# The block compression of a hybrid decoder's first mixer: blocks stationary in four column quarters, weights moving

## The chip, the cores and the metric

The kernel runs on one core of one Trainium2 chip. The core has a matrix engine (TensorE, PE in the profile, whose weight loads are listed as PEld), a vector engine (VectorE, DVE), a scalar engine (ScalarE, ACT), GpSimd (POOL) and a queue engine (SyncE, SP) that issues the DMA transfers. The metric is the device time of one execution in microseconds (us). Everything is computed in float32.

## The reference

Two layers over 256 tokens of width 1024. Layer 0 mixes with RWKV-7 heads and sparse-attention heads side by side, layer 1 with Mamba-2; each is followed by a mixture of 32 experts. The change is in layer 0, in the compressed branch of the sparse attention. It turns overlapping blocks of 32 tokens (a new block each 16 tokens, so 15 blocks) of the key and of the value columns into one vector each, by a two-layer network:

```python
n_cmp = (s_ - CMP_BLOCK) // CMP_STRIDE + 1        # 15
blk_idx = np.arange(n_cmp)[:, None] * CMP_STRIDE + np.arange(CMP_BLOCK)[None, :]

def compress(t, pe, w1, b1, w2):
    blocks = kv_heads(t)[:, blk_idx] + pe[:, None, :]
    flat = blocks.transpose(0, 1, 3, 2, 4).reshape(b_, n_cmp, hk, CMP_BLOCK * d)
    return jax.nn.silu(flat @ w1 + b1) @ w2       # w1: 2048 x 128, w2: 128 x 64

k_cmp = partial_rope(compress(kc, pe_k, w1_k, b1_k, w2_k), cmp_end)
v_cmp = compress(vc, pe_v, w1_v, b1_v, w2_v)
```

`flat @ w1` is a contraction over 32 positions `l` of a block times 64 channels, for 2 KV heads times 15 blocks = 30 rows and 128 hidden units, once for keys and once for values.

## The kernel before

The program of each engine is written out by hand, one after another, in blocks for the first mixer ("hyb"), the experts, the second mixer ("ssm") and the experts again. Engines meet only at semaphores: `at(...)` is the count that a named mark has reached. PSUM banks are taken in turn: `take(pe, ..., pool=left)` hands out banks 0 to 3 in rotation, and waits until the bank's last job has been read. `right` is the other four banks ("sums" in the profile).

In the first mixer the input projection is cut into six groups of columns. Their weights pass through two halves of `wr`, each refilled by the SP queue when the group two before it is done (mark `("group", g)`). `by_channels` (line 1140) computes 256 columns of a group, with the weights stationary and the 256 tokens of `uT` moving: 16 products over 8 steps. The second half of group 3 (`("feat", NK, 1)`) is written out apart, since it is mixed with the compression.

The compression's operands: `w1` holds the first-layer weights as [64 channels, l, 128], keys on partitions 0 to 63 (`x` = 0), values on 64 to 127 (`x` = 1); it lies in `front`, under which name the profile shows it. `blk` holds the blocks plus their position terms as [64 channels, l, 30], laid out likewise, and is made by four additions on VectorE. For each of the 32 positions and both `x` one product has `w1` of the position stationary (64 rows, 128 columns) and the 30 columns of `blk` moving, accumulated in one bank for each `x` as [128 hidden, 30]. After each pair of positions stands one of the 16 products of the projection (line 1189). ScalarE then applies the sigmoid and the bias (lines 994 and 996, `hsg` and `hid`), VectorE multiplies the two (line 698), and PE multiplies by `w2` (line 1207), behind the low-rank products of line 1200. ScalarE's copy of the projection's bank into `z` (line 932) stands behind lines 994 and 996 in its queue.

What follows in the mixer is one long chain on PE, VectorE and ScalarE. The expert weights come through a ring of slots, `raw`; the SP queue loads ahead into it wherever the mixer's own tiles have been given up (`load_ahead`), after waits for marks of the mixer.

Of the kernel before, what the change touches and what calls it, by code (L numbers as in the profile page):

```python
# [11 lines left out]
ACT = mybir.ActivationFunctionType  # L12
AX = mybir.AxisListType

P = 128
D = 1024
SEQ = 256
HALVES = SEQ // P
KD = D // P
# [4 lines left out]
HEADS, HD = 8, 64  # L24
# [3 lines left out]
KV = 2  # L28
# [5 lines left out]
NCMP, CBLK, CSTR = 15, 32, 16  # L34
# [24 lines left out]
def columns(spec):  # L59

    at, out = 0, {}
    for name, n in spec:
# [4 lines left out]


CHK = 64
NCHK = SEQ // CHK  # L70
LEVELS = range(1, 6)

# [1 line left out]
                         ("ident64", CHK), ("slots", 128), ("slots_s", 128), ("key", 32),  # L74
                         ("headones", 2), ("headsum", 32), ("headspread", 512), ("scankeep", 256), ("strict_upto", 2 * CHK),
                         ("causal", 256), ("cmpok", 30), ("cos", 16), ("sin", 16), ("ccos", 8), ("csin", 8),
                         ("lev0", CHK), ("levT", 6 * CHK)])

SHARED = CONST["headones"][0]

# [9 lines left out]
def shape_tables():  # L90
    c = np.zeros((P, NCONST), np.float32)

    def put(name, v):
        at, n = CONST[name]
        c[:, at:at + n] = v.reshape(P, n)

    i = np.arange(P)
    put("ident", np.eye(P))
    put("before", (i[:, None] < i[None, :]).astype(np.float32))
    put("upto", (i[:, None] <= i[None, :]).astype(np.float32))  # L100
    put("ones", np.ones((P, P)))
    head = np.arange(HEADS)
    put("headones", (i[:, None] // HD == np.arange(2)[None, :]).astype(np.float32))
    put("headsum", np.stack([head[None, :] == 2 * m + i[:, None] // HD for m in range(4)], 1).astype(np.float32))
    spread = np.zeros((P, 4, P), np.float32)
    for m in range(4):
        spread[:HEADS, m, :] = head[:, None] == 2 * m + i[None, :] // HD
    put("headspread", spread)
    loc, pos = i[:, None] % CHK, np.arange(CHK)
    put("ident64", (loc == pos[None, :]).astype(np.float32))  # L110
    put("strict_upto", np.concatenate([loc < pos[None, :], loc <= pos[None, :]], 1).astype(np.float32))
    put("slots", np.tile(np.arange(P) % CAP, (P, 1)))
    put("slots_s", np.tile(np.arange(P) % CAP_S, (P, 1)))
    e = np.arange(EXPERTS)
    put("key", np.tile(np.maximum(FIXED - e, 0) * FIRST_KEY - e, (P, 1)))
    put("scankeep", np.tile((np.arange(SEQ) % CHK != 0), (P, 1)))
    put("causal", np.concatenate([np.zeros((P, P)), np.where(i[None, :] <= i[:, None], 0, NEG)], 1))
    tok = i[:, None] + P * np.arange(HALVES)[None, :]
    end = np.arange(NCMP) * CSTR + CBLK - 1
    put("cmpok", (end[None, None, :] <= tok[:, :, None]).astype(np.float32))  # L120
    inv = np.power(np.float32(500000.0), -np.arange(ROPE_HALF, dtype=np.float32) * np.float32(2.0 / 16))
    ang = tok[:, :, None].astype(np.float32) * inv
    put("cos", np.cos(ang)), put("sin", np.sin(ang))
    cang = np.zeros((P, ROPE_HALF), np.float32)
    cang[:NCMP] = end[:, None].astype(np.float32) * inv
    put("ccos", np.cos(cang)), put("csin", np.sin(cang))
    lev = np.stack([(loc >> (l + 1) == pos[None, :] >> (l + 1)) & (loc >> l & 1 == 1)
                    & (pos[None, :] >> l & 1 == 0) for l in range(6)], 1).astype(np.float32)
    put("lev0", lev[:, 0])
    put("levT", np.tile(lev[:CHK].transpose(2, 1, 0), (2, 1, 1)))  # L130
    return c

# [15 lines left out]
def build(nc, a, known, new):  # L148
# [3 lines left out]
    pe_done, act_done, dve_done, pool_done = sem("pe_done"), sem("act_done"), sem("dve_done"), sem("pool_done")  # L152
    sems = {"pe": pe_done, "act": act_done, "dve": dve_done, "pool": pool_done}
    E = {k: Count(k, new) for k in sems}
    PE, AC, DV, PO = E["pe"], E["act"], E["dve"], E["pool"]

    def at(*mark):

        who, n = known.get(mark, ("pe", 1))
        return sems[who], n  # L160
# [11 lines left out]
    def C(name, rows=P):  # L172
        o, n = CONST[name]
        return cst[0:rows, o:o + n] if o < SHARED else cst_hyb[0:rows, o - SHARED:o - SHARED + n]

    def FT(name, rows=P):
        o, n = FEAT[name]
        return feat[0:rows, o:o + n]
# [8 lines left out]
    def take(pe, *job, pool=tuple(range(8))):  # L187

        n = turn["n"].get(pool, 0)
        turn["n"][pool] = n + 1  # L190
        b = pool[n % len(pool)]
        if turn["last"][b] is not None:
            pe.wait_ge(*at("read", *turn["last"][b]))
        turn["last"][b] = job
        new[("bank",) + job] = ("pe", b)
        return bank[b]

    def bank_of(*job):
        return bank[known.get(("bank",) + job, ("pe", 0))[1]]
# [224 lines left out]
    hyb = Area(AREA)  # L424
# [5 lines left out]
    cT = hyb("cT", [P, KV, SEQ])  # L430
    w2 = hyb("w2", [P, 2, HD])
    pe_ = hyb("pe_", [P, CBLK])
    blk = hyb("blk", [P, CBLK, KV * NCMP])
    hid, hsg = hyb("hid", [P, 2, KV * NCMP]), hyb("hsg", [P, 2, KV * NCMP])
    cmpk = hyb("cmpk", [NCMP, KV, 2, HD])
    crp = hyb("crp", [NCMP, 4, 2 * KV * ROPE_HALF])
# [34 lines left out]
    uT = hyb("uT", [P, KD, SEQ])  # L471
# [6 lines left out]
    amt, dcy = R4("amt"), R4("dcy")  # L478
    wr = hyb("wr", [P, 2, KD, BANK])
    cst_hyb = hyb("cst_hyb", [P, NCONST - SHARED])  # L480

    flat = lambda ap, *dims: ap.rearrange("p " + " ".join(dims) + " -> p (" + " ".join(dims) + ")")
    u = front[:, 0:2 * D].rearrange("p (t d) -> p t d", t=HALVES)
    junk = front[:, 3 * D:4 * D]
    w1 = front[:, :].rearrange("p (l m) -> p l m", m=P)
# [47 lines left out]
    with nc.Block(name="hyb", no_gpsimd_drain=True) as block:  # L533
# [44 lines left out]
        def _(dve):  # L578
# [90 lines left out]
            nc.vector.memset(eps_n[:, 2:3], 1e-5)  # L669
            nc.vector.memset(eps_n[:, 3:4], 0.0)  # L670
            nc.vector.memset(z[:, :, 0:1], 0.0)
            nc.vector.memset(zlo[:, :, 0:1], 0.0).then_inc(dve_done, DV.one(("consts",)))
            dve.wait_ge(s_ld["ident"], 16)
            dve.wait_ge(s_ld["x"], 16)
# [93 lines left out]
            lev0, levT = C("lev0"), C("levT").rearrange("p (l s) -> p l s", s=CHK)  # L768
# [123 lines left out]
            for t in range(HALVES):  # L892
                rows = slice(0, P) if t else slice(CHK, P)
# [25 lines left out]
        def _(act):  # L919
            A = nc.scalar  # L920
# [8 lines left out]
            def columns_read(g, j):  # L929

                act.wait_ge(*at("feat", g, j))
                A.copy(z[:, 4 * g + 2 * j:4 * g + 2 * j + 2, 1:SEQ + 1],
                       bank_of("feat", g, j)[:, :].rearrange("p (c t) -> p c t", c=2)).then_inc(
                    act_done, AC.one(("read", "feat", g, j)))
# [25 lines left out]
            for t in range(HALVES):  # L960
                act.wait_ge(*at("nsa", 1, t))
                b = bank_of("nsa", 1, t)
# [17 lines left out]
            for br in range(2):  # L980
# [8 lines left out]
            A.activation(gts[:, :, :], nsav[:, :, 4 * HD:4 * HD + 24], ACT.Sigmoid).then_inc(act_done,  # L989
                                                                                          AC.one(("gates",)))  # L990
            columns_read(NK, 0)
            for x, n in enumerate("kv"):
                act.wait_ge(*at("hid", "mm", x))
                A.activation(hsg[:, x, :], bank_of("hid", "mm", x)[:, 0:KV * NCMP], ACT.Sigmoid,
                             bias=FT("b1_" + n)).then_inc(act_done, AC.one())
                A.activation(hid[:, x, :], bank_of("hid", "mm", x)[:, 0:KV * NCMP], ACT.Identity,
                             bias=FT("b1_" + n)).then_inc(act_done, AC.one(("hsg", x)))
                new[("read", "hid", "mm", x)] = ("act", AC.n)
            columns_read(NK, 1)
            act.wait_ge(*at("zz", 7))  # L1000
            for c in range(4):
                i = A.activation(kk2[:, c, :], k4[:, c, :], ACT.Square, scale=FT("k_k")[:, c:c + 1])
            i.then_inc(act_done, AC.one(("kk2",)))
            for name, dst, bias in (("wup", dcy, "w0"), ("aup", amt, "a0")):
                for j in range(2):
                    act.wait_ge(*at(name, j))
                    for c in (2 * j, 2 * j + 1):
                        A.activation(dst[:, c, :], bank_of(name, j)[:, (c % 2) * SEQ:(c % 2 + 1) * SEQ], ACT.Sigmoid,
                                     bias=FT(bias)[:, c:c + 1]).then_inc(
# [105 lines left out]
        def _(pe):  # L1115
            T = nc.tensor
            left, right = (0, 1, 2, 3), (4, 5, 6, 7)
# [46 lines left out]
            for x, (o, m) in enumerate(LO):  # L1164
                b = take(pe, "lo", x, pool=left)
                for k in range(KD):
                    i = T.matmul(b[0:m, 0:SEQ], wr[:, 0, k, o:o + m], uT[:, k, :], start=(k == 0), stop=(k == KD - 1))
# [7 lines left out]
                turned(("kT", br), [two(t, HEADS + 4 * br + 2 * g) for g in range(KV) for t in range(HALVES)], left)  # L1175
            by_channels(3, NK, 0)
            pe.wait_ge(*at("blk", 1, 1))
            bs = [take(pe, "hid", "mm", x, pool=left) for x in range(2)]
            w = weights(3)
            b = take(pe, "feat", NK, 1, pool=left)  # L1180
            for l in range(CBLK):
                for x in range(2):
                    i = T.matmul(bs[x][:, 0:KV * NCMP], w1[HD * x:HD * x + HD, l, :], blk[HD * x:HD * x + HD, l, :],
                                 start=(l == 0), stop=(l == CBLK - 1))
                    if l == CBLK - 1:
                        i.then_inc(pe_done, PE.one(("hid", "mm", x)))
                if l % 2:
                    c, step = divmod(l // 2, KD)
                    i = T.matmul(b[:, c * SEQ:(c + 1) * SEQ], w[:, step, (2 + c) * P:(3 + c) * P], uT[:, step, :],
                                 start=(step == 0), stop=(step == KD - 1))  # L1190
            i.then_inc(pe_done, PE.one(("feat", NK, 1)))
            new[("group", 3)] = ("pe", PE.n)
            pe.wait_ge(*got("par"))
# [1 line left out]
            for x, name in enumerate(("wup", "aup")):  # L1195
                lo = slice(W_RANK * x, W_RANK * (x + 1))
                for j in range(2):
                    b = take(pe, name, j, pool=right)
                    for c in (2 * j, 2 * j + 1):
                        i = T.matmul(b[:, (c % 2) * SEQ:(c % 2 + 1) * SEQ], par[lo, c * P:(c + 1) * P], lo3[lo, 0, :],  # L1200
                                     start=True, stop=True)
                    i.then_inc(pe_done, PE.one((name, j)))
            pe.wait_ge(*at("hid", 1))
            b = take(pe, "cmp", pool=left)
# [6 lines left out]
            b = take(pe, "ksum", pool=right)  # L1211
# [1639 lines left out]
```

## Time and profile before

| | |
|---|---|
| median of 3 runs | 1397.82 us (1396.78 to 1404.53) |
| the profiled execution | 1401.55 us |
| its span, first to last instruction | 1399.7 us |
| mean granted TensorE clock (1 is full) | 0.959 |
| PE busy | 1272.6 us, 91% of the span |
| DVE, ACT busy | 410.1 us, 269.3 us |
| moved by DMA | 464.10 MB, mean 332 GB/s |

The profile was taken of one execution, the runs are others; the profiled one was 3.7 us above the median. A float32 product shows as two records of PE (MATMUL) and two of PEld (LDWEIGHTS). A form such as "64*128 64x30" is the stationary operand (rows * columns), then the moving one (rows x columns). A record's own time is its latency, and the records of a run overlap: the rate at which PE works is read from where one group of records starts and the next one does.

### The profile page before, as it was taken

How to read it: one execution, taken by the hardware profiler on the slowest of the kernel's cores; microseconds unless marked ns; L12 is line 12 of the kernel's file. 1: busy time of each engine (PE TensorE's matmuls, PEld its weight loads, DVE VectorE, ACT ScalarE, POOL GpSimd, SP SyncE). 2: the span in 40 equal slices, each digit the busy share in tenths (PEclk: the TensorE clock that was granted, in tenths of full speed). 3: DMA queues.
4: the chain of work that ended last, by engine and by line, in shares of the span. 5: the costliest groups of instructions: out<-in, count | busy, mean ns of one | idle time of the engine just before them, and what ended most of it. 6: DMA issues, size and time to landing. Idle time of an engine off the chain costs nothing. (4 is left out here: it accounts for less than half of the span.)

```text
span 1399.7 us, 21009 instructions
## 1 busy us (share of the span) xinstructions
PE 1272.6 (91%) x8852; PEld 717.3 (51%) x8852; DVE 410.1 (29%) x1024; ACT 269.3 (19%) x535; POOL 15.2 (1%) x18
## 2 busy tenths in 40 slices
PE   6999999899999988698989999998999999876986
PEld 3668896544444334253368788535444444333432
DVE  1236775421211211012035756315211211110212
ACT  2223341211011000010131566202111110000101
POOL 0000000000000000000000101000000000000000
PEclk9999999999999989989999999999999999997999
DMA  9511107999999999999965446757999999999996
GB/s 305 181 61 61 62 5 298 407 409 428 426 427 428 427 427 427 424 427 427 389 228 202 150 169 253 316 231 306 430 427 427 428 427 427 427 427 424 427 428 262
DMA packets 63484, 464.10 MB, mean 332 GB/s; under 512 B 8272, under 2 KB 13680, under 8 KB 34960
## 3 DMA queue, kind: packets, MB, share of 16 engines
q1 hardware_dynamic: 63376, 462.59, 80.8%
q8 instruction: 76, 1.25, 0.4%
q14 instruction: 32, 0.26, 0.0%
HBM read 461.50 MB, written 1.08 MB: 330 GB/s over the span
## 5 line engine op out<-in xcount | busy, mean ns | idle before, releaser
L1974 PE MATMUL bank<-raw,xg 128*32 128x512 f32 x1664 | 234.7, 656 | 45.3 <-DMA raw<-in_moe_w_up 39.2
L1884 DVE TENSOR_TENSOR aT<-bank,sg 128x128 f32<-128x128 f32 (+1 forms) x64 | 20.3, 317 | 558.4 <-ACT sg L1795 558.4
L1974 PEld LDWEIGHTS bank<-raw,xg 128*32 128x32 f32 x1664 | 57.6, 119 | 196.7 <-issue 123.7
L1911 PE MATMUL bank<-sel,ux 128*128 128x64 f32 (+1 forms) x896 | 118.2, 288 | 16.9 <-DVE sel L1817 12.0
L1911 PEld LDWEIGHTS bank<-sel,ux 128*128 128x128 f32 x896 | 111.0, 202 | 40.9 <-issue 26.0
L2021 PE MATMUL sums<-ys,selT 64*128 64x512 f32 x512 | 127.2, 615 | 3.3 <-DVE ys L1897 3.3
L1792 ACT COPY gus<-bank 128x512 f32<-128x512 f32 x64 | 37.5, 586 | 436.6 <-PE bank L1974 331.4
L2012 PE MATMUL bank<-raw,aT 128*32 128x512 f32 x832 | 100.0, 598 | 10.8 <-DVE aT L1884 10.8
L2021 PEld LDWEIGHTS sums<-ys,selT 64*128 64x128 f32 x512 | 44.0, 186 | 87.6 <-issue 80.7
L1955 PE MATMUL bank<-raw,xg 128*64 128x512 f32 x384 | 84.8, 594 | 0.0
L2615 PE MATMUL sums<-uT,wr 128*128 128x256 f32 x352 | 78.1, 380 | 0.0
L1897 DVE COPY ys<-bank 128x512 f32<-128x512 f32 x64 | 44.0, 688 | 111.6 <-PE bank L2012 79.8
L1985 PEld LDWEIGHTS bank<-cst,gus 128*128 128x128 f32 x416 | 50.3, 191 | 44.5 <-issue 34.9
L2615 PEld LDWEIGHTS sums<-uT,wr 128*128 128x128 f32 x352 | 66.3, 190 | 9.4 <-issue 0.7
L1985 PE MATMUL bank<-cst,gus 128*128 128x64 f32 x416 | 57.5, 281 | 4.2 <-ACT gus L1792 4.2
L1766 ACT COPY xg<-bank 128x256 f32<-128x256 f32 (+1 forms) x56 | 23.4, 418 | 178.3 <-PE bank L1911 178.3
L2615 PE MATMUL bank<-uT,wr 128*128 128x256 f32 x256 | 57.1, 381 | 0.0
L1955 PEld LDWEIGHTS bank<-raw,xg 128*64 128x64 f32 x384 | 27.5, 137 | 51.7 <-issue 50.7
L2615 PEld LDWEIGHTS bank<-uT,wr 128*128 128x128 f32 x256 | 48.0, 190 | 6.9 <-issue 0.7
L2012 PEld LDWEIGHTS bank<-raw,aT 128*32 128x32 f32 x832 | 21.7, 109 | 50.6 <-issue 30.4
L1999 PE MATMUL bank<-raw,aT 128*64 128x512 f32 x192 | 43.8, 599 | 3.0 <-DVE aT L1884 3.0
L1795 ACT ACTIVATE sg<-bank 128x128 f32<-128x128 f32 (+1 forms) x64 | 19.1, 298 | 137.7 <-PE bank L1985 114.8
(415 smaller groups left out, 1326.6 us busy)
## 6 DMA issues: line engine op xcount, KB each, us to landing
raw<-in_moe_w_gate SPq DMA_DIRECT2D x54, 2048.0 KB, 40.8
raw<-in_moe_w_up SPq DMA_DIRECT2D x54, 2048.0 KB, 45.3
raw<-in_moe_w_down SPq DMA_DIRECT2D x54, 2048.0 KB, 44.7
raw<-in_moe_w_gate SPq DMA_DIRECT2D x20, 1024.0 KB, 12.5
raw<-in_moe_w_up SPq DMA_DIRECT2D x20, 1024.0 KB, 13.5
raw<-in_moe_w_down SPq DMA_DIRECT2D x20, 1024.0 KB, 13.5
wr<-in_ssm_w_in SPq DMA_DIRECT2D x10, 2048.0 KB, 8.7
wr<-in_hyb_w_in SPq DMA_DIRECT2D x5, 2048.0 KB, 7.7
```

The costliest lines, as they stand in the source:

```text
L1766: nc.scalar.copy(dst[:, :, 4 * half:4 * half + 4, :].rearrange("p x k s -> p k x s"), bank[SIDE_BANK][:, 0:8 * n].rearrange("p (k x s) -> ...
L1792: nc.scalar.copy(gus[:, :, :], bank[GU_BANK][:, :].rearrange("p (q j) -> p j q", j=4)).then_inc(S["gus"], 1)
L1884: V.tensor_tensor(out, bank[TURN_BANK][:, 0:8 * n].rearrange("p (j x) -> p j x", j=4)[:, :, n:2 * n], gated, ALU.mult).then_inc(S["act"], 1)
L1897: V.tensor_copy(ys[:, :], bank[Y_BANK][:, :]).then_inc(S["y"], 1)
L1911: i = T.matmul(bank[SIDE_BANK][:, k * n:(k + 1) * n].rearrange("p (x s) -> p x s", x=2), ux[:, t, 4 * half + k, :], src[:, t, :, :], start ...
L1955: i = T.matmul(bank[GU_BANK][CAP * m:CAP * m + CAP, :], xg[:, odd, k, :], raw[:, slot, (k % 4) * FH:(k % 4 + 1) * FH], start=(k == 0), sto ...
L1974: i = T.matmul(bank[GU_BANK][CAP_S * c:CAP_S * c + CAP_S, :], xg_f[:, x, 4 * half + k, :], raw[:, slot, k * FH:(k + 1) * FH], start=(half ...
L1985: i = T.matmul(bank[TURN_BANK][:, j * CAP:(j + 1) * CAP], gus[:, j, :], C("ident64"), start=True, stop=True)
L1999: i = T.matmul(bank[Y_BANK][CAP * n:CAP * n + CAP, :], aT[:, j, :], raw[:, slot, jj * D + n * BANK:jj * D + (n + 1) * BANK], start=(j == 0 ...
L2012: i = T.matmul(bank[Y_BANK][CAP_S * c:CAP_S * c + CAP_S, :], aT_s[:, 2 * half + jj, :], raw[:, slot, jj * D + n * BANK:jj * D + (n + 1) * ...
L2021: i = T.matmul(bank[ACC[2 * t + n]][:, :], selT[CAP * n:CAP * n + CAP, x, t * P:(t + 1) * P], ys[CAP * n:CAP * n + CAP, :], start=False, s ...
L2615: i = T.matmul(b[:, c * SEQ:(c + 1) * SEQ], wr2[:, n % 3, k, (2 * j + c) * P:(2 * j + c + 1) * P], uT2[:, k, :], start=(k == 0), stop=(k = ...
```

## The change

The compression's two operands change places. A block matrix (64 rows, now 32 columns: 30 and two columns of zeros) is stationary, and the 128 columns of `w1` of the position move. Position `l` goes to the quarter `l % 4` of the output partitions, that is of the array's columns, so each quarter gathers 8 of the 32 positions as [32 blocks, 128 hidden]. ScalarE copies the two banks to `hid4`, and for each `x` one product of `hid4` (stationary, 128 x 128) with `fold`, four identities of 32 stacked (128 x 32), adds the quarters and turns the result to [128 hidden, 32]. The 16 products of the projection no longer stand between those of the compression: all 64 of these come first, then 8 of the projection, the two folding products, and the other 8.

```diff
+BLK = 32
-                         ("lev0", CHK), ("levT", 6 * CHK)])
+                         ("lev0", CHK), ("levT", 6 * CHK), ("fold", BLK)])
+    put("fold", (i[:, None] % BLK == np.arange(BLK)[None, :]).astype(np.float32))
-    blk = hyb("blk", [P, CBLK, KV * NCMP])
+    blk = hyb("blk", [P, CBLK, BLK])
+    hid4 = hyb("hid4", [P, 2, P])
+            nc.vector.memset(blk[:, :, KV * NCMP:BLK], 0.0)
...
             columns_read(NK, 0)
+            act.wait_ge(*at("hid", "parts"))
+            for x in range(2):
+                A.copy(hid4[:, x, :], bank_of("hid", "part", x)[:, 0:P]).then_inc(
+                    act_done, AC.one(("read", "hid", "part", x)))
+            act.wait_ge(*at("hid", "mm"))
             for x, n in enumerate("kv"):
-                act.wait_ge(*at("hid", "mm", x))
-                A.activation(hsg[:, x, :], bank_of("hid", "mm", x)[:, 0:KV * NCMP], ACT.Sigmoid,
-                             bias=FT("b1_" + n)).then_inc(act_done, AC.one())
-                A.activation(hid[:, x, :], bank_of("hid", "mm", x)[:, 0:KV * NCMP], ACT.Identity,
-                             bias=FT("b1_" + n)).then_inc(act_done, AC.one(("hsg", x)))
-                new[("read", "hid", "mm", x)] = ("act", AC.n)
+                folded = bank_of("hid", "mm")[:, BLK * x:BLK * x + KV * NCMP]
+                A.activation(hsg[:, x, :], folded, ACT.Sigmoid, bias=FT("b1_" + n)).then_inc(act_done, AC.one())
+                A.activation(hid[:, x, :], folded, ACT.Identity, bias=FT("b1_" + n)).then_inc(
+                    act_done, AC.one(("hsg", x)))
+            new[("read", "hid", "mm")] = ("act", AC.n)
             columns_read(NK, 1)
...
             pe.wait_ge(*at("blk", 1, 1))
-            bs = [take(pe, "hid", "mm", x, pool=left) for x in range(2)]
+            bs = [take(pe, "hid", "part", x, pool=left) for x in range(2)]
+            for l in range(CBLK):
+                q = slice(BLK * (l % 4), BLK * (l % 4) + BLK)
+                for x in range(2):
+                    rows = slice(HD * x, HD * x + HD)
+                    i = T.matmul(bs[x][q, 0:P], blk[rows, l, :], w1[rows, l, :], start=(l < 4), stop=(l >= CBLK - 4))
+            i.then_inc(pe_done, PE.one(("hid", "parts")))
             w = weights(3)
             b = take(pe, "feat", NK, 1, pool=left)
-            for l in range(CBLK):
-                for x in range(2):
-                    i = T.matmul(bs[x][:, 0:KV * NCMP], w1[HD * x:HD * x + HD, l, :], blk[HD * x:HD * x + HD, l, :],
-                                 start=(l == 0), stop=(l == CBLK - 1))
-                    if l == CBLK - 1:
-                        i.then_inc(pe_done, PE.one(("hid", "mm", x)))
-                if l % 2:
-                    c, step = divmod(l // 2, KD)
-                    i = T.matmul(b[:, c * SEQ:(c + 1) * SEQ], w[:, step, (2 + c) * P:(3 + c) * P], uT[:, step, :],
-                                 start=(step == 0), stop=(step == KD - 1))
+            for c in range(2):
+                for k in range(KD):
+                    i = T.matmul(b[:, c * SEQ:(c + 1) * SEQ], w[:, k, (2 + c) * P:(3 + c) * P], uT[:, k, :],
+                                 start=(k == 0), stop=(k == KD - 1))
+                if c == 0:
+                    pe.wait_ge(*at("read", "hid", "part", 1))
+                    f = take(pe, "hid", "mm", pool=left)
+                    for x in range(2):
+                        i = T.matmul(f[:, BLK * x:BLK * x + BLK], hid4[:, x, :], C("fold"), start=True, stop=True)
+                    i.then_inc(pe_done, PE.one(("hid", "mm")))
```

PE's program at the compression before the change. A row gives the line, the operation, the tiles written and read, and the output's shape; L1140 is the first half of group 3, L1183 the compression, L1189 the second half, and the pair of rows L1183 and L1189 stands 16 times.

```order
L1140 MATMUL bank<-uT,wr 128x256 x16
L1183 MATMUL bank<-blk,front 128x30 x4
L1189 MATMUL bank<-uT,wr 128x256
...
L1200 MATMUL sums<-lo_99,par 128x256 x8
L1207 MATMUL bank<-w_101,hid 15x64 x4
L1213 MATMUL sums<-exc,cst_hyb 8x256 x4
```

The same place in the changed program, where L1191 is the compression, L1197 the projection, L1203 the folding, and the following rows are the old L1200, L1207 and L1213.

```order
L1148 MATMUL bank<-uT,wr 128x256 x16
L1191 MATMUL bank<-front,blk 32x128 x64
L1197 MATMUL bank<-uT,wr 128x256 x8
L1203 MATMUL bank<-cst_hyb,hid_148 128x32 x2
L1197 MATMUL bank<-uT,wr 128x256 x8
L1214 MATMUL sums<-lo_99,par 128x256 x8
L1221 MATMUL bank<-w_101,hid 15x64 x4
L1227 MATMUL sums<-exc,cst_hyb 8x256 x4
```

The 64 products of the compression now stand in one piece instead of 16, and the projection's 16 in two pieces; nothing behind them moved.

ScalarE's program at the same place, before.

```order
L932 COPY z<-bank 128x2x256
L994 ACTIVATE hsg<-bank,feat 128x30
L996 ACTIVATE hid<-bank,feat 128x30
L994 ACTIVATE hsg<-bank,feat 128x30
L996 ACTIVATE hid<-bank,feat 128x30
L932 COPY z<-bank 128x2x256
L1002 ACTIVATE exc<-zz,feat 128x256 x4
```

And in the changed program.

```order
L936 COPY z<-bank 128x2x256
L998 COPY hid_148<-bank 128x128 x2
L1003 ACTIVATE hsg<-bank,feat 128x30
L1004 ACTIVATE hid<-bank,feat 128x30
L1003 ACTIVATE hsg<-bank,feat 128x30
L1004 ACTIVATE hid<-bank,feat 128x30
L936 COPY z<-bank 128x2x256
L1010 ACTIVATE exc<-zz,feat 128x256 x4
```

Two copies are new ahead of the four activations. VectorE has one more small instruction, a fill of `blk` at its start. The SP queue has the same transfers in the same order behind the same waits; only the one table transfer that brings `fold` is wider, 1744 columns for 1712.

## Rows read from the trace of the kernel before

**Rows 1.** The page's part 1, and its DMA slices (busy tenths of 40).

```profile
PE 1272.6 (91%) x8852; PEld 717.3 (51%) x8852; DVE 410.1 (29%) x1024; ACT 269.3 (19%) x535; POOL 15.2 (1%) x18
DMA  9511107999999999999965446757999999999996
```

**Rows 2.** Stretches (us): length, busy by engine, clock, DMA share, GB/s.

```profile
60.00:68.00 8.00, 8.00 (x45) 6.89 (x43) 0.72 (x2) 5.44 (x9) 0.00 (x0) 1.00 0.75 264
68.00:87.04 19.04, 19.04 (x161) 13.10 (x160) 1.60 (x4) 1.11 (x5) 0.00 (x0) 1.00 0.00 1
87.04:96.00 8.96, 7.46 (x36) 4.12 (x35) 7.05 (x19) 6.66 (x16) 0.00 (x0) 0.72 0.68 235
230.00:700.00 470.00, 424.71 (x2692) 194.31 (x2692) 94.92 (x288) 52.98 (x120) 0.00 (x0) 0.96 1.00 421
```

**Rows 3.** What the SP queue waited for up to 260 us: total, times, longest.

```profile
SPq L293 <- PE bank L1189: 27.4, 1, 27.4
SPq L373 <- PE sums L1287: 21.6, 1, 21.6
SPq L373 <- DVE mixn L647: 13.4, 1, 13.4
```

**Rows 4.** PE's timeline at the compression: start, duration, group, count, idle before.

```profile
60.96 7.07 PE L1140 MATMUL bank<-uT,wr 128*128 128x256 f32 x32
67.97 0.63 PE L1183 MATMUL bank<-blk,front 64*128 64x30 f32 x8
68.53 0.70 PE L1189 MATMUL bank<-uT,wr 128*128 128x256 f32 x2
69.16 0.63 PE L1183 MATMUL bank<-blk,front 64*128 64x30 f32 x8
...
86.42 0.70 PE L1189 MATMUL bank<-uT,wr 128*128 128x256 f32 x2
87.05 2.96 PE L1200 MATMUL sums<-lo,par 32*128 32x256 f32 x16
...
92.05 3.57 PE L1213 MATMUL sums<-exc,cst_hyb 128*8 128x256 f32 x8 [1.50 <-ACT dcy L1008]
```

**Rows 5.** PE's timeline at other places, where tiles of other shapes run.

```profile
104.76 1.96 PE L1280 MATMUL bank<-kcT,qT 64*128 64x15 f32 x32
136.26 1.98 PE L1309 MATMUL sums<-front,qk 64*64 64x128 f32 x64
...
186.59 1.10 PE L1346 MATMUL sums<-kp,kk 64*64 64x64 f32 x32
187.52 1.10 PE L1346 MATMUL sums<-kk,kp 64*64 64x64 f32 x32
...
204.61 3.71 PE L1431 MATMUL sums<-wr,kk 64*64 64x128 f32 x64
...
306.59 3.62 PE L1974 MATMUL bank<-raw,xg 128*32 128x512 f32 x32
...
312.05 1.10 PE L1985 MATMUL bank<-cst,gus 128*128 128x64 f32 x8
312.99 1.95 PE L1911 MATMUL bank<-sel,ux 128*128 128x64 f32 x16
```

**Rows 6.** ScalarE's timeline behind the compression.

```profile
86.52 0.29 ACT L994 ACTIVATE hsg<-bank,feat 128x30 f32<-128x30 f32 x1 [17.86 <-PE bank L1183]
...
87.04 0.29 ACT L996 ACTIVATE hid<-bank,feat 128x30 f32<-128x30 f32 x1
87.21 0.60 ACT L932 COPY z<-bank 128x512 f32<-128x512 f32 x1
```

**Rows 7.** The page's group of ScalarE reads of 128 columns: busy, mean ns.

```profile
L1795 ACT ACTIVATE sg<-bank 128x128 f32<-128x128 f32 (+1 forms) x64 | 19.1, 298 | 137.7 <-PE bank L1985 114.8
```

**Rows 8.** Two-us stretches of PE: length, busy, clock, DMA share, GB/s.

```profile
92.00:94.00 2.00, 1.95 (x5) 0.50 1.04 401
98.00:100.00 2.00, 2.00 (x11) 1.00 0.00 0
```

## The prediction

> **What bounds the kernel now.** Three views were read in turn: the page for the whole, the stretches for each stage, and PE's timeline for the place of the change. The page has PE busy for 91% of the span and DMA busy at nine tenths or more from the seventh slice to the twentieth, and again in the last twelve [rows 1]. So the experts are DMA's: from 230 to 700 us its share is 1.00 at 421 GB/s [rows 2]. The change lies before that, in the first mixer, where between 68 and 87 us PE is busy in each of the 19.04 us, DMA moves nothing, and VectorE and ScalarE have 1.60 and 1.11 us of work [rows 2]. PE alone sets the time there.
>
> Does a gain there reach the end? The SP queue shows it. The refill of `wr` for the last group waits 27.4 us for line 1189; the first load-ahead waits 21.6 us for line 1287, the large one 13.4 us for `mixn`, a late result of the mixer [rows 3]. Each transfer behind the change is released by work behind the change, so the whole DMA-bound stage starts earlier by what the mixer gains, and ends earlier by as much. The hybrid weights of group 4 came in the stretch from 60 to 68 us (DMA share 0.75) and wait for nothing here [rows 2]; needed some 8 us sooner, they are still there. I count the carry at 1 us per us.
>
> **What is removed.** The mixed piece runs from 67.97 to 87.05 us, 19.08 us [rows 4]. One of its 16 periods is 69.16 - 67.97 = 1.19 us: 8 records of the compression and 2 of the projection. The projection alone goes at (67.97 - 60.96) / 32 = 219 ns a record of 256 columns [rows 4], so 0.44 us of a period are its own. The remaining 0.75 us are the compression and the changes between the tile shapes 64*128 and 128*128. Line 1280 has the same stationary shape with half the moving columns, 32 records in 1.96 us, 61 ns each at most [rows 5]. Eight of those are 0.49 us, and 0.26 us are left for two changes of shape. So the 19.08 us are about 7.0 of projection, 7.8 of compression and 4.2 of shape changes.
>
> **What is added, on PE.**
>
> The projection in two pieces: 16 products, 32 records, 7.01 us as in its first half.
>
> Two changes of shape, into the compression and out of it: 0.26 us. The folding products have the projection's shape, 128*128, and cause none.
>
> The folding: 2 products, 4 records with 128 stationary columns. The nearest rows are line 1985's, 8 records in 312.99 - 312.05 = 0.94 us, 118 ns each [rows 5]: 0.47 us. Its wait is covered: ScalarE has two copies of 128 columns, 298 ns each by its reads of that size [rows 7], 0.6 us in all, while PE has 8 products of the projection, 3.5 us. Without that cover some 0.8 us would be bare, if hand-overs of 0.1 us are allowed for at each end.
>
> The compression: 64 products, 128 records, stationary 64*32, moving 64x128. No such shape is in the trace, so its rate is bounded. Moving 128 columns takes 219 / 2 = 110 ns in one tile. How many tiles run at once is to be read from the rows that move 128 columns or more [rows 5]. Line 1431 uses only the diagonal, two tiles of 64*64: 3.71 us / 64 = 58 ns. Line 1309 uses four: 1.98 / 64 = 31 ns at most. Line 1974 has four column quarters over all 128 rows, as the change has them, and moves 512 columns in 3.62 / 32 = 113 ns, where one tile alone would need 438. So quarters do run beside each other, nearly four at a time. Eight tiles would give 110 / 8 = 14 ns. The loading of weights sets the other bound: 61 ns for 128 columns (line 1280), 187.52 - 186.59 = 0.93 us / 32 = 29 ns for 64 (line 1346), which halved gives 15 ns for 32. Both bounds from below agree at about 15 ns, but no record in these rows follows another in less than 29 ns, and I can't tell from them whether something else holds them there. I take the nearest fastest row, 29 ns: 128 x 29 = 3.7 us. Ends: 15 ns, 1.9 us, and 58 ns, 7.4 us.
>
> The Trainium skill ("TensorE: Matmul & The Clock Gate", Part 1, the section on 56 and 53.3 ns) states that starts of matmuls never come closer than about 25 ns, however little they move; its estimate for this piece would be 128 x 25 = 3.2 us and the saving 8.1 us. No row here goes below that figure, and none is narrow enough to test it.
>
> **Sum.** 7.01 + 0.26 + 0.47 + 3.7 = 11.4 us for 19.08: 7.6 us less. It is made against the profiled execution, 1401.55 us with a span of 1399.7, which would become 1393.9; the median of the runs is 3.7 us lower, 1397.82, and becomes 1390.2.
>
> **Edits at nothing.** ScalarE's copy into `z` now starts 0.1 us behind the projection's end, since the four activations before it in the queue are done during the last 3.5 us of projection; before, they ended at about 87.3, just where the copy was ready [rows 6], so this is worth 0.1 us at most. VectorE's product of `hid` and `hsg` comes earlier, and line 1207, which needs it, stood behind 2.96 us of line 1200 anyway [rows 4]. The fill of two columns of `blk` is a small instruction at the start, while VectorE waits for its first data; uncovered it would cost a few tenths. The table is 16 KB wider, 0.04 us at 421 GB/s. One more bank of the left four is taken, so later jobs use other banks; the job whose read each must await is four takes back as before, except for the next few, whose banks were read several us earlier. The idle 1.50 us ahead of line 1213 [rows 4] hangs on ScalarE's chain from the projection's end and stays.
>
> **Rivals.**
>
> *Only the two row groups overlap.* Successive products alternate between rows 0 to 63 and 64 to 127, and if quarters of the same rows waited for each other, two would run at once, as on line 1431: 58 ns, 7.4 us. Saving 3.9 us, 1393.9. Line 1974 speaks against it, with its 113 ns for 512 columns. The Trainium skill (same page, Part 3, on what overlaps) has exactly this rule: a weight load overlaps matmuls in flight only where the row group differs. By line 1974, whose four quarters share all rows, the trace disagrees. 12%.
>
> *Loading at its own rate.* The records follow at 15 ns: 1.9 us, saving 9.4 us, 1388.4. For it: 61 and 29 ns scale with the columns loaded. Against it: no row below 29. 20%.
>
> *The clock falls.* The granted clock is 1.00 over the mixed piece, and 0.72 over the 9 us behind it, which hold the idle 1.5 us and the thin products of line 1213 [rows 2, 4]. It was at the lower level, 1.2 of 2.4 GHz, at 92 to 94 and back at 98 to 100 us [rows 8]. A piece with small tiles, without the 256-column products in between, could bring the same on, and then the projection behind it runs at half speed for up to 7.5 us, 3.7 us lost: 1393.9. Against it: lines 1309 and 1346 run tiles at similar filling, four 64*64 tiles at 31 and 29 ns, and line 1309's time is that of the full clock. 10%.
>
> *Slower: the tiles don't overlap at all,* because the two records of one product meet in the same small tile. Then a record costs its 110 ns, the compression 14.1 us, and the piece 21.8 us instead of 19.08: 2.7 us longer, 1400.5. It decides from 11.3 / 128 = 89 ns a record; for over 0.5% it takes 143 ns, as with the lower clock on top (220 ns, 28 us, 1414.6). Lines 1974 and 1309 speak against it: their products have two records too. 5%.
>
> *The gain is local.* If what follows gave it back, about 1397.8. For it only that later work waits for DMA; against it, that the DMA itself waits for the mixer [rows 3]. 5%.
>
> **How the numbers follow.** The forecast, 29 ns and 1390.2, has the remaining 48%; the run scatter (two of three runs 1 us apart, one 7 us above) adds about 1.5 us on either side. The range from 1386.5 to 1395.5 takes in the bounds of the rate, 1388.4 and 1393.9, and the clock's case, and leaves out the slower, the local one and the odd high run. A measurement of this kernel tells about 0.5% from no change, which is 7.0 us: the forecast's 7.6 lies just beyond it. I count 7 in 10 of the forecast and nearly all of the fast case as faster, 0.54; the slower case splits between slower and no change, with a little for unforeseen loss, 0.05; the rest, 0.41, is within 0.5%.
>
> **What would show it.** In the changed profile: line 1191 with 128 records from about 68.0, the projection's first record 3.7 to 4.0 us later; line 1203 with no idle time before it; line 1214 starting at about 79.4 instead of 87.05; clock 1.00 up to there; the first load-ahead issued some 7.6 us earlier, and the same distance between it and the end. The forecast is wrong if line 1191 takes under 3 or over 5 us, if PE waits before line 1203, or if the distance from line 1214 to the end has changed by more than a few us, for which the clock's low stretches later in the mixer would be the first suspect.

## The result and the profile after

The changed kernel takes 1389.76 us (median of 8 runs, 1387.35 to 1392.96); the kernel before, in 8 runs beside it, 1399.32 us (1396.78 to 1404.53). The ratio is 0.9936, with a 95% interval of 0.9923 to 0.9948: faster by 9.0 us, 7.3 to 10.8; the two medians as they stand are 9.6 us apart. A second comparison on another occasion gave 1389.71 against 1398.18, ratio 0.9926 (0.9910 to 0.9943).

The profiled execution took 1387.79 us, with a span of 1386.0 us and a mean clock of 0.966. Part 1 of the page, its DMA slices, and the stretch of the change, which answer to [rows 1, 2]:

```profile
PE 1259.3 (91%) x8856; PEld 710.9 (51%) x8856; DVE 410.1 (30%) x1025; ACT 269.6 (19%) x537; POOL 15.2 (1%) x18
DMA  9520118999999999999964455858999999999996
```

```profile
68.67:78.18 9.51, 9.51 (x166) 8.21 (x165) 1.96 (x5) 1.83 (x7) 0.00 (x0) 1.00 0.01 2
```

PE's timeline at the compression (start, duration, group, count, idle before), the answer to [rows 4]:

```profile
68.67 2.03 PE L1191 MATMUL bank<-front,blk 64*32 64x128 f32 x128
70.62 3.72 PE L1197 MATMUL bank<-uT,wr 128*128 128x256 f32 x16
74.18 0.53 PE L1203 MATMUL bank<-cst_hyb,hid 128*128 128x32 f32 x4
74.55 3.70 PE L1197 MATMUL bank<-uT,wr 128*128 128x256 f32 x16
78.18 2.96 PE L1214 MATMUL sums<-lo,par 32*128 32x256 f32 x16
81.07 0.62 PE L1221 MATMUL bank<-w,hid 128*15 128x64 f32 x8
83.11 3.14 PE L1227 MATMUL sums<-exc,cst_hyb 128*8 128x256 f32 x8 [1.43 <-ACT dcy L1016]
```

The piece from the compression's first record to the low-rank products is 78.18 - 68.67 = 9.51 us, where it was 19.08 [rows 4]: 9.57 us less. The 128 records stand in 1.95 us, 15.2 ns each, the change of shape behind them included. Line 1203 has no idle time before it, and costs 74.55 - 74.18 = 0.37 us. ScalarE's timeline shows why nothing waits:

```profile
70.75 0.43 ACT L998 COPY hid<-bank 128x128 f32<-128x128 f32 x2 [1.39 <-PE bank L1191]
74.75 0.29 ACT L1003 ACTIVATE hsg<-bank,feat 128x30 f32<-128x30 f32 x1 [3.57 <-PE bank L1203]
...
78.28 0.58 ACT L936 COPY z<-bank 128x512 f32<-128x512 f32 x1 [2.72 <-PE bank L1197]
```

The copies are done at 71.18, 3 us before the folding wants them, and the copy into `z` starts as soon as the projection ends.

The two profiled executions differ by 13.7 us in their spans, more than the medians. The large load-ahead divides them (SP queue of the changed kernel; before, the same transfer was issued at 223.52):

```profile
212.23 0.33 SPq L375 DMA_DIRECT2D raw<-in_moe_w_gate  x1
```

Up to the compression the changed kernel's execution was 0.70 us later; the compression's piece gave 9.57; from there to this load it took 134.05 us for 136.47, 2.4 less; and from the load to the end 1173.8 for 1176.2, again 2.4 less. The last two are not steps of the change: the programs are the same there, and the second profiled execution of the changed kernel (changed_again, below) took 136.53 us from the piece's end to this load and 1176.5 from there, the same as the kernel before, and had a span of 1390.7. The 9.57 us of the piece are what the medians show, 9.6 us.

### The profile page after: what moved, and what is told of

Its sections match the earlier page's. It is cut to its first block and busy times, and to the rows that moved or that the text cites. A ratio compares the mean times of both kernels' runs of the same rounds, so it can differ in the third digit from the quotient of the medians.

```text
span 1386.0 us, 21021 instructions
## 1 busy us (share of the span) xinstructions
PE 1259.3 (91%) x8856; PEld 710.9 (51%) x8856; DVE 410.1 (30%) x1025; ACT 269.6 (19%) x537; POOL 15.2 (1%) x18
## 3 DMA queue, kind: packets, MB, share of 16 engines
q8 instruction: 76, 1.25, 0.4%
```

## The experiments

Theory A: the products run beside each other in as many tiles as there are row groups times column quarters, so a record costs its moving time over the number of tiles, and that is most of the gain. Rival B: the gain is the end of the mixing with the projection, and the swap of the operands adds little. Two further questions: what sets the 15 ns, and whether a us here is a us at the end. Where no time is given below, the kernel ran once, for its trace, and only the piece is compared.

**one_piece.** The kernel before, its 64 products of the old form in one piece, the projection behind:

```diff
             for l in range(CBLK):
                 for x in range(2):
                     i = T.matmul(bs[x][:, 0:KV * NCMP], w1[...], blk[...], ...)
-                if l % 2:
-                    c, step = divmod(l // 2, KD)
-                    i = T.matmul(b[:, c * SEQ:(c + 1) * SEQ], w[:, step, ...], uT[:, step, :], ...)
+            for c in range(2):
+                for step in range(KD):
+                    i = T.matmul(b[:, c * SEQ:(c + 1) * SEQ], w[:, step, ...], uT[:, step, :], ...)
```

> The kernel of before with one edit: its 64 products of the compression (w1 stationary 64*128, 30 columns moving) stand in one piece, and the 16 of the projection behind them. Theory A (the swap of the operands into eight tiles is the gain): the piece of PE from the first product of the compression to the low-rank ones takes 128 x 59 ns + 0.26 + 7.01 = 14.8 us, so 4.2 us of the 9.6 come from taking the products apart (15 pairs of shape changes at 0.28 us) and 5.4 us from the swap; run 1395 against 1399. Rival B (the mixing was the cost, the swap adds little): the piece takes about 10 us, as in the changed kernel, and the run 1390.

Measured: 1397.46 us (12 runs) against 1399.09 (17), ratio 0.9988 (0.9978 to 0.9999). PE's timeline, and its stretches (length, busy, clock, DMA share, GB/s):

```profile
67.95 8.51 PE L1181 MATMUL bank<-blk,front 64*128 64x30 f32 x128
76.38 9.29 PE L1189 MATMUL bank<-uT,wr 128*128 128x256 f32 x32
85.60 2.96 PE L1200 MATMUL sums<-lo,par 32*128 32x256 f32 x16
```

```profile
70.00:72.00 2.00, 2.00 (x42) 1.00 0.00 0
72.00:74.00 2.00, 2.00 (x40) 0.97 0.00 0
74.00:76.00 2.00, 2.00 (x22) 0.50 0.04 8
...
76.38:85.60 9.22, 9.22 (x34) 0.77 0.00 0
```

The piece took 17.65 us, not 14.8. After some 6 us of nothing but 30-column products the clock fell to its lower level of 1.2 GHz, and the projection behind them took 9.22 us where it takes 7.01. So B is refuted as the whole of the gain: taking the products apart, with the old operands, is worth 1.4 us in this trace and 1.6 in the medians. It saves the shape changes and gives most of that back through the clock. With the projection's products between the compression's the clock had stayed at 1.00 over the whole piece [rows 2]. What the end of the mixing is worth beside the swap is worked out behind mixed, below.

**one_strip, two_strips.** The changed kernel with one or two column quarters, that is two or four tiles (`n` is 1 or 2):

```diff
-                q = slice(BLK * (l % 4), BLK * (l % 4) + BLK)
+                q = slice(BLK * (l % n), BLK * (l % n) + BLK)
...
-                        i = T.matmul(f[...], hid4[:, x, :], C("fold"), ...)
+                        i = T.matmul(f[...], hid4[0:BLK * n, x, :], C("fold", BLK * n), ...)
```

> The changed kernel with all 32 positions in the first column quarter (output partitions 0 to 31); the folding then only turns 32 rows. Only the two row groups can run beside each other. Theory (time per record = moving time of one tile, 107 to 110 ns, over the tiles that run at once): 54 ns a record, 6.9 us for the 128. Rival (the rate is set by the loading of 32 columns, and the quarters don't matter): 15 ns, 2.0 us.

> The changed kernel with the positions in two column quarters (l % 2), four tiles in all. Theory of tiles at once: 27 ns a record, 3.5 us for the 128. Rival (loading alone sets the rate): 15 ns, 2.0 us.

PE's timeline of one_strip, then of two_strips:

```profile
68.86 7.18 PE L1191 MATMUL bank<-front,blk 64*32 64x128 f32 x128
75.96 3.72 PE L1197 MATMUL bank<-uT,wr 128*128 128x256 f32 x16
```

```profile
67.91 3.70 PE L1191 MATMUL bank<-front,blk 64*32 64x128 f32 x128
71.54 3.72 PE L1197 MATMUL bank<-uT,wr 128*128 128x256 f32 x16
```

7.10 and 3.63 us, so 55.5 and 28.4 ns a record, and 15.2 with all four quarters. Twice the tiles, half the time. Theory A holds, and the loading of 32 columns does not set the rate.

**moving_half, narrow_both, narrow_stationary.** What sets the 15 ns: half the moving columns, half of both, or half the stationary columns. Each of the three leaves out part of the layer, so only their times are of use.

```diff
-                    i = T.matmul(bs[x][q, 0:P], blk[rows, l, :], w1[rows, l, :], ...)
+                    i = T.matmul(bs[x][q, 0:64], blk[rows, l, :], w1[rows, l, 0:64], ...)         # moving_half
+                    i = T.matmul(bs[x][q16, 0:64], blk[rows, l, 0:16], w1[rows, l, 0:64], ...)    # narrow_both
+                    i = T.matmul(bs[x][q16, 0:P], blk[rows, l, 0:16], w1[rows, l, :], ...)        # narrow_stationary
```

> The changed kernel with only 64 of the 128 hidden units moved (the other half of the compression's first layer is left out). Moving time is halved, loading of 32 columns is as before. If the moving columns over eight tiles set the 15 ns: 7 to 8 ns a record, about 1 us for the 128. If the loading of weights (32 columns, two row groups) or the issue of a record sets them: 15 ns, 2.0 us.

> The changed kernel with 64 of 128 hidden units moved and only 16 of the 32 columns of a block matrix stationary (the rest is left out). Both moving and loading are halved. If 15 ns is a time of issue per record: still 15 ns, 2.0 us for the 128. If it is loading: 7 to 8 ns, 1.0 us. The 25 ns that the Trainium skill (TensorE: Matmul & The Clock Gate, Part 1) gives as the least distance of two starts would be 3.2 us; the changed kernel's 15.2 ns are already below it.

> The changed kernel with only 16 of the 32 columns of a block matrix stationary (the rest of the blocks is left out), all 128 columns moved. If the moving columns over eight tiles set the changed kernel's 15.2 ns: 15 ns again, 1.95 us for the 128 records. If the loading of weights sets it: nearer to the 11 ns that the halved moving gave.

PE's timelines of the three, in this order:

```profile
68.03 1.48 PE L1192 MATMUL bank<-front,blk 64*32 64x64 f32 x128
69.44 3.72 PE L1198 MATMUL bank<-uT,wr 128*128 128x256 f32 x16
```

```profile
68.58 1.43 PE L1192 MATMUL bank<-front,blk 64*16 64x64 f32 x128
69.94 3.72 PE L1198 MATMUL bank<-uT,wr 128*128 128x256 f32 x16
```

```profile
67.95 2.00 PE L1191 MATMUL bank<-front,blk 64*16 64x128 f32 x128
69.88 3.72 PE L1197 MATMUL bank<-uT,wr 128*128 128x256 f32 x16
```

11.0, 10.6 and 15.1 ns a record. Loading fewer columns changes nothing; moving fewer does, from 15.2 to 11.0, but not by half, and with both halved it stays near 10.6. So the 15 ns are moving time (110 / 8 = 14; from start to start the changed kernel's records are 13.9 ns apart, the rest is the change of shape behind them), and close below lies something that none of these sizes moves. The start times in moving_half's trace show it setting in: the first 32 records are 7.7 ns apart, near to the 55 / 8 = 7 of the theory, those behind the fortieth 9.8.

**tile_by_tile.** The same products, one quarter after another instead of in rotation:

```diff
-            for l in range(CBLK):
+            for l in [4 * i + j for j in range(4) for i in range(CBLK // 4)]:
```

> The changed kernel with the same 64 products and tiles, in another order: first all positions of quarter 0, then of quarter 1, and so on; the two row groups still alternate. If PE takes its matmuls in the order of the program and one waits where its tile is busy, only two tiles run at once: 54 ns a record, 6.9 us for the 128. If it can take later products whose tiles are free ahead of it: about 15 ns, 2.0 us.

```profile
68.52 5.98 PE L1191 MATMUL bank<-front,blk 64*32 64x128 f32 x128
74.43 3.72 PE L1197 MATMUL bank<-uT,wr 128*128 128x256 f32 x16
```

5.91 us, 46 ns a record, three times the rotated order. The order in the program decides. It is less than one_strip's 7.10 with its single quarter, so some products of the next quarter do start early; by what rule, this run doesn't tell.

**mixed.** Eight of the projection's products back between those of the compression, one behind each eight of them:

```diff
+                if l % 4 == 3:
+                    k = l // 4
+                    i = T.matmul(b[:, 0:SEQ], w[:, k, 2 * P:3 * P], uT[:, k, :], start=(k == 0), stop=(k == KD - 1))
```

> The changed kernel with eight of the projection's 16 products put between those of the compression, one behind each eight of them, so seven pairs of shape changes more; the folding stands in the middle of the other eight. If a pair of changes costs 0.26 to 0.28 us, as worked out from the kernel of before: the piece up to the low-rank products takes 9.5 + 7 x 0.27 = 11.4 us. If the cost belonged to the wide stationary operand alone and not to the change of shape: 9.5 us.

PE's timeline, two of the eight periods and the start of the low-rank products:

```profile
67.96 0.45 PE L1193 MATMUL bank<-front,blk 64*32 64x128 f32 x16
68.34 0.70 PE L1196 MATMUL bank<-uT,wr 128*128 128x256 f32 x2
68.97 0.45 PE L1193 MATMUL bank<-front,blk 64*32 64x128 f32 x16
...
79.93 2.96 PE L1216 MATMUL sums<-lo,par 32*128 32x256 f32 x16
```

11.97 us for 9.51: seven more pairs of changes cost 2.46 us, 0.35 us a pair. "Mode switching requires drain", as the Trainium skill has it ("TensorEngine Tiling (Array Packing)", Key Properties). The time lost at each pair here agrees with that.

With this the 9.57 us of the piece can be shared out. The old products, while the clock is full, start in pairs 112 ns apart in one_piece's trace, 56 ns a record: 7.2 us for the 128, where the new ones take 1.95, so 5.2 us less. A period of before, 1.19 us, then holds 0.45 us of compression, 0.44 of projection and 0.30 for its pair of shape changes; 15 pairs fewer are 4.5 us. The folding costs 0.37. Together that is some 9.4 of the 9.57 us. So the faster records are a little over half of the gain, and the end of the mixing, which brought one_piece only 1.4 us, is nearly the other half once the piece is too short for the clock to fall in it. The swap with all 16 pairs of changes left in was not run; by the 0.35 us a pair it is estimated at 9.51 + 15 x 0.35 = 14.8 us, 4.3 less than before.

**nine_times.** The carry to the end, by an addition:

```diff
-            for l in range(CBLK):
+            for l in list(range(CBLK)) * 9:
```

> The changed kernel with its 64 products of the compression issued nine times over (the last time counts), 1024 records more on PE at 15.2 ns, 15.6 us. If a us in this piece is a us at the end: 15.6 us above the changed kernel's 1389.8, so 1405.4, ratio to before 1.0043. Rival (the mixer's end is partly covered by transfers, or the gain is local): clearly less, 1390 to 1398. If a long piece of small tiles lowers the clock, the records go at 30 ns for part of it and the run is above 1408.

Measured: 1417.02 us against 1399.09, ratio 1.0132 (1.0117 to 1.0148), 27.3 us above the changed kernel's 1389.76. PE's timeline:

```profile
68.55 3.91 PE L1191 MATMUL bank<-front,blk 64*32 64x128 f32 x263
73.52 2.02 PE L1191 MATMUL bank<-front,blk 64*32 64x128 f32 x128 [1.06 <-issue]
77.26 2.02 PE L1191 MATMUL bank<-front,blk 64*32 64x128 f32 x128 [1.72 <-issue]
...
97.84 3.72 PE L1197 MATMUL bank<-uT,wr 128*128 128x256 f32 x16
```

Both numbers of the expectation were wrong, and the question is answered all the same. The piece took 29.29 us instead of 1.95, 27.3 more, and the run is 27.3 us longer: one us per us, with some 2 us either way by the interval. The clock did not fall. But after 263 records PE stood idle before each next 128, for 1.06 us the first time and 1.72 us each time after, with nothing to wait for in the program.

**in_the_gap, changed_again.** A version that might beat both: the compression behind the low-rank products, where PE stood idle for 1.43 us; folding behind the head sums, the product with `w2` between the halves of the next projection, ScalarE's and VectorE's parts later in their queues. Beside it the changed kernel as it is.

```diff
             T.matmul(...)                     # wup, aup
+            # the 64 products of the compression
             T.matmul(...)                     # ksum
+            # the folding; first half of by_channels(4, NR, 0); the products with w2; second half; kcT
```

> The changed kernel with the compression moved behind the low-rank products, where PE stood idle 1.4 us for ScalarE; the folding comes behind the head sums, the product with w2 between the two halves of the next projection, the last turn behind them, and ScalarE's and VectorE's parts stand later in their queues accordingly. If the idle time can be filled: 1.4 us of the compression's 2.0 us disappear, and if the lower clock that followed the idle time stays away too, 1 to 3 us more: 1385 to 1388 for the changed kernel's 1389.8. Rival: ScalarE, with the two copies now between its sigmoids, sets the time of the folding, PE waits there instead, and the run is within 1 us of the changed kernel's.

> The changed kernel itself, for a comparison on the same chip: 1389.8 us, ratio to before 0.9936 within its interval of 0.9923 to 0.9948.

Measured: in_the_gap 1387.53 us (1385.15 to 1389.55), ratio 0.9923 (0.9910 to 0.9936); changed_again 1389.71, ratio 0.9926 (0.9910 to 0.9943). The medians are 2.2 us apart; the two intervals lie on each other, so a gain over the changed kernel is not shown. PE's timeline of in_the_gap:

```profile
74.88 2.96 PE L1201 MATMUL sums<-lo,par 32*128 32x256 f32 x16
77.78 3.64 PE L1210 MATMUL bank<-front,blk 64*32 64x128 f32 x128
81.35 1.89 PE L1215 MATMUL sums<-exc,cst_hyb 128*8 128x256 f32 x8
```

The idle time before the head sums is gone, and PE did not wait before the folding. But in this execution the clock was at 0.50 from 78 to 80 us, though PE had never been idle behind the projection's start, and the compression took 3.57 us for 1.95. There is also a new wait of 0.55 us, for ScalarE's copy into `z`, which stands behind more work in its queue:

```profile
92.31 0.71 PE L1253 MATMUL bank<-kT,qT 64*128 64x128 f32 x8 [0.55 <-ACT z L936]
```

## Why the prediction was right, and where it was off

*The place and the carry: right.* PE alone set the time of the piece, and a us here is a us at the end: shown by nine_times with 27.3 for 27.3, and by the change itself, 9.57 us in the piece and 9.6 in the medians.

*The time: 1390.2 forecast, 1389.76 measured.* That it came within 0.5 us is luck: two errors cancel. Against three runs of before I forecast 7.6 us less; measured it is 9.0 (7.3 to 10.8), 9.6 by the medians and 9.57 in the piece, and the kernel before moved up by 1.5 us when more runs were added.

*The step that was off is the rate of the compression,* 29 ns a record, 3.7 us; it was 15.2 ns, 1.95 us, below the 3 us that I had named as a sign of a wrong forecast. It is the case I gave 20% as "loading at its own rate". The rate came from the sentence that no record in the rows follows another in less than 29 ns. Line 1346, from which it came, is no floor: its products use rows and columns of the same half, so only the diagonal's two tiles of 64*64 run at once, and 64 moving columns take 55 / 2 = 27 ns by the moving time, 29 in the row. I saw this for line 1431 and overlooked it for line 1346, also where the clock's rival calls its tiles four. And the trace of before has line 1321, with the same shape in all four tiles, which the prediction did not use:

```profile
128.06 1.16 PE L1321 MATMUL sums<-qk,front 64*64 64x64 f32 x64
129.16 1.13 PE L1140 MATMUL bank<-uT,wr 128*128 128x256 f32 x4
```

64 records in 1.10 us are 17 ns each, the change of shape included, where moving time over tiles gives 55 / 4 = 14. With this row the forecast would have been moving time over tiles, 14 ns, and a saving of 9.5 us. The reason given for that case was wrong as well: not the columns loaded (narrow_stationary, 15.1 ns with half of them) but those moved set the 15 ns. The estimate of 3.2 us from the Trainium skill's least distance of about 25 ns ("TensorE: Matmul & The Clock Gate", Part 1) was too long; this trace has 15.2, and narrow_both 10.6. Line 1321's 17 ns were below it already in the trace of before, so the prediction's remark that no row goes below it holds only for the rows it used.

*Shape changes: 0.26 us a pair assumed;* some 0.30 for the old shapes, since the old records took 56 ns and not the 61 of line 1280, and 0.35 for the small tiles in mixed. The compression before was 7.2 us and not 7.8. *Folding: 0.47 us forecast, 0.37 measured,* hidden wait right. *ScalarE, VectorE, table, banks at nothing:* right; no new wait appears.

*The rivals.* Only the row groups overlap: refuted by the change, and one_strip shows what it would have been, 55.5 ns. No overlap at all: refuted. The gain is local: refuted. The clock falls: it did not, in four quarters; but the fear was not empty, since with the old operands in one piece (one_piece) it does, and some 3 us are lost that way. So taking the products apart needs the swap beside it. Alone it gains 1.6 us; with the operands swapped and the tiles in rotation, the compression is over in 2 us, and the clock stays at 1.00 through the whole piece.

*Not forecast well:* the distance from line 1214 to the end. In the profiled executions it shrank by 4.8 us. As the suspect I named the low stretches of the clock, and these differ between executions of the same instructions: line 1227 took 3.14 us here and 3.57 in changed_again, at a clock of 0.50, and 1.89 in narrow_stationary at 1.00:

```profile
82.37 1.89 PE L1227 MATMUL sums<-exc,cst_hyb 128*8 128x256 f32 x8 [1.43 <-ACT dcy L1016]
```

The distance itself goes with the clock: among the ten profiled executions of the changed kernel and its variants that keep the order behind line 1214, it is 1305.2 to 1308.0 us in the five with a mean clock of 0.965 or more, 1310.9 in mixed at 0.964, and 1310.1 to 1313.0 in the four at 0.961 or less, with changed_again the longest of all. The kernel before, at 0.959, has 1312.7, and changed_again, at a like clock, 1313.0: nothing shows the 4.8 us to be part of the change. That the clock is their whole cause was not shown.

## What to carry to other kernels

For small products, divide the moving time of a record in one tile by the number of tiles that the order of the program keeps busy; then put consecutive products into different tiles, since the same products tile by tile took three times as long. Before a row serves as a floor, look at which tiles its line addresses. When short products are taken out from between long ones, count the shape changes saved, 0.30 to 0.35 us a pair here, and look at the granted clock over the thin stretch that results: it fell in one_piece, whose stretch was 8 us long, and did not in the changed kernel with 2 us of it.

## What the runs showed of the hardware that was not expected

Records of eight 64*32 tiles follow each other at 15.2 ns with 128 columns moved, 11.0 with 64, the change of shape behind them included.

A long run of such records outruns something that feeds PE: in nine_times 263 records went at full speed, then each further 128 took 2.02 us of work and 1.72 us of idle time without a releaser, 29 ns a record. The page of that run has 84 packets and 1.38 MB in the queue of instructions, the changed kernel 76 and 1.25: 8 packets of 16 KB more for 1024 more records, one for each 128. In nine_times' trace these packets start 3.5 to 3.8 us apart, at 71.15, 74.64, 78.39, 82.12 us and so on, and take 0.9 to 1.3 us; the stops end at 73.52, 77.26, 81.00 and 84.73, each 1.3 to 1.5 us behind the end of a packet. That the stops are PE waiting for its instructions follows from this match in number and time, and no run varied it.

The clock fell to its lower level in one_piece after some 6 us of 30-column products with PE never idle, and in in_the_gap at the start of the compression, behind 10 us of projection and low-rank products. In nine_times, with PE idle for 11.4 of the 29.3 us, it stayed at 1.00 throughout. In these runs the clock did not follow PE's busy time.
